# Transposing attention probabilities in halves of 64 queries, and taking the value products one pair of heads later

## The reference

```python
for i in range(S // BLOCK):                      # two blocks of 128 queries
    q0, e = i * BLOCK, (i + 1) * BLOCK
    s = jnp.einsum('bqhd,bkhd->bhqk', q[:, q0:e], k[:, :e]) * scale
    s = s + c[:, :, q0:e, None] - c[:, :, None, :e]        # a bias for each head
    p = jax.nn.softmax(jnp.where(causal, s, NEG), axis=-1)
    outs.append(jnp.einsum('bhqk,bkhd->bqhd', p, v[:, :e]))
# y = concat(ya * silu(ga), yb * silu(gb));  x + y @ w_out
```

## Time and profile before

| | |
|---|---|
| median of 3 runs | 768.49 us (768.45 to 770.68) |
| profiled execution | 769.24 us, span 767.4 us |
| PE busy | 759.1 us of the span, 99% |
| DVE, ACT, POOL busy | 69%, 54%, 29% |
| granted TensorE clock | 0.998 of full speed |
| the two stretches of `attend_gated` | about 121.6 to 140.1 us and 215.5 to 233.9 us |
| attention of the third layer | about 521 to 539 us |

### The profile page before, as it was taken

One profiled execution on the slowest core, in us unless ns is written; L12 is line 12 of the kernel. 1 busy time (PEld: TensorE's weight loads), 2 busy tenths in 40 slices (PEclk: granted clock), 3 DMA queues, 4 the chain that ended last, 5 costly groups with the idle time before them and its releaser, 6 DMA issues.

```text
span 767.4 us, 12161 instructions
## 1 busy us (share of the span) xinstructions
PE 759.1 (99%) x4802; PEld 647.4 (84%) x4802; DVE 528.3 (69%) x793; ACT 417.4 (54%) x678; POOL 222.7 (29%) x175
## 2 busy tenths in 40 slices
PE   9999999999999999999999999999999999999997
PEld 7888887899877889887778888998888888888885
DVE  5876876755577557975567865788788676667553
ACT  6675458443696454453344554727857555456451
POOL 2113993730940000064029900126012111011010
PEclk9999999999999999999999999999999999999999
DMA  8989886578622745455435565430465656655741
GB/s 263 234 191 270 266 191 181 128 178 198 157 62 81 240 141 193 160 197 161 141 110 164 193 219 167 142 133 29 163 194 158 184 174 199 196 189 165 244 167 55
DMA packets 79064, 131.98 MB, mean 172 GB/s; under 512 B 4656, under 2 KB 28496, under 8 KB 79008
## 3 DMA queue, kind: packets, MB, share of 16 engines
q1 hardware_dynamic: 77072, 126.01, 55.9%
q0 software_dynamic: 1648, 5.09, 2.3%
q10 hardware_dynamic: 288, 0.11, 0.1%
HBM read 130.12 MB, written 1.06 MB: 171 GB/s over the span
## 4 chain that ended last, share of the span: by engine, by line
PE 98%; DVE 1%; issue 0%; ACT 0%; DVEq 0%; ACTq 0%
PE ps L1765 16%; PE ps L1769 15%; PE ps L1773 15%; PE ps L1840 10%; PE ps L1822 7%; PE ps L1848 5%; PE ps L1827 3%; PE ps L1806 3%; PE ps L1810 3%; PE ps L1802 3%; PE ps L1915 2%; PE ps L1931 2%; PE ps L1946 2%; PE ps L2304 1%; PE ps L2181 1%; PE ps L2133 1%
## 5 line engine op out<-in xcount | busy, mean ns | idle before, releaser
L1067 DVE TENSOR_TENSOR w_lo<-stage,w_hi 128x1024 fp32r<-128x1024 f32 x224 | 292.3, 1330 | 136.9 <-ACT w_hi L688 136.0
L688 ACT ACTIVATE w_hi<-stage 128x1024 fp32r<-128x1024 f32 x230 | 239.2, 1060 | 213.5 <-PE ps L1773 103.7
L1765 PE MATMUL ps<-w_hi,act_t 128*128 128x512 f32 (+1 forms) x368 | 100.5, 396 | 0.2 <-ACT act_t L715 0.2
L1773 PE MATMUL ps<-w_lo,act_t 128*128 128x512 f32 (+1 forms) x368 | 96.5, 385 | 0.0
L1840 PE MATMUL ps<-act_t,w_hi 128*128 128x512 f32 x352 | 84.1, 391 | 0.0
L1773 PEld LDWEIGHTS ps<-w_lo,act_t 128*128 128x128 f32 x368 | 68.1, 188 | 14.0
L1769 PE MATMUL ps<-w_hi,act_t 128*128 128x512 f32 (+1 forms) x304 | 79.4, 384 | 0.0
L1765 PEld LDWEIGHTS ps<-w_hi,act_t 128*128 128x128 f32 x368 | 66.5, 188 | 15.1 <-issue 2.5
L1840 PEld LDWEIGHTS ps<-act_t,w_hi 128*128 128x128 f32 x352 | 64.7, 188 | 12.7
L1769 PEld LDWEIGHTS ps<-w_hi,act_t 128*128 128x128 f32 x304 | 56.1, 188 | 11.6
L1822 PE MATMUL ps<-act_t,w_hi 128*128 128x512 f32 x224 | 56.5, 394 | 0.0
(11 more groups left out here) (399 smaller groups left out, 1248.3 us busy)
## 6 DMA issues: line engine op xcount, KB each, us to landing
stage<-in_even_w_in SPq DMA_DIRECT2D x62, 512.0 KB, 5.4
stage<-in_odd_w_in SPq DMA_DIRECT2D x48, 512.0 KB, 4.5
stage<-in_w_gate_up SPq DMA_DIRECT2D x44, 512.0 KB, 4.7
stage<-in_w_down SPq DMA_DIRECT2D x22, 512.0 KB, 4.3
stage<-in_even_w_out SPq DMA_DIRECT2D x16, 512.0 KB, 4.4
stage<-in_odd_w_out SPq DMA_DIRECT2D x16, 512.0 KB, 4.0
stage<-in_w_in SPq DMA_DIRECT2D x10, 512.0 KB, 3.7
stage<-in_w_out SPq DMA_DIRECT2D x8, 512.0 KB, 4.7
```

The lines of the kernel that those rows point to most:

```text
L688: nc.scalar.activation(w_hi[:, u % RING, :], stage[:, u % RING, :], ACT.Copy).then_inc(hi_ready, 1)
L1067: nc.vector.tensor_tensor(w_lo[:, u % RING, :], stage[:, u % RING, :], w_hi[:, u % RING, :].bitcast(F32), ALU.subtract).then_inc(lo_ready, 1)
L1765: mm(out[:, b, :], a_hi(k)[:, tok[b]], hi[:, i, :], start=(k == 0), stop=False)
L1773: ins = mm(out[:, b, :], a_hi(k)[:, tok[b]], lo[:, i, :], start=False, stop=(k == k_tiles - 1))
```

## The change

Each transpose of 128 queries is cut into two of 64 queries: rows 0 to 63 and rows 64 to 127 of the slot are the weights of two transposes in the 64*128 division, the one that the scores use, and they land in two banks side by side. Both heads of a pair share these two banks. One copy then takes both heads of a pair (768 columns, `slots_of_pair` from `turned_pair`) on one engine: ACT has pairs 3, 5 and 7 of a half and DVE the other five; in the third layer ACT has pairs 0 and 2, DVE pairs 1 and 3. The order in `attend_gated` becomes: turn pair i, scores of pair i+4, values of pair i-2. The gates' transposes keep their place behind the scores, and so now stand behind the turning of the same step. There are eight slots instead of six, and the tile `wf_both` moves into the shared work area to make room.

```diff
-SLOTS = 6
+SLOTS = 8
-COPIED_BY_ACT = (1, 3, 5, 7, 9, 13, 15)
+PAIRS_BY_ACT = (3, 5, 7)
@@ sizes and places
-            return (6 if n < FOX_H + DIL_H and n % 16 < 2 else 2) + n % 2
+            return 6 if n < FOX_H + DIL_H and n % 16 < 2 else 2
+        def turned_half(n, m, h):
+            at = (turned_at(n) + h) * BANK + m * 192
+            return ps[:, at:at + 192].rearrange("p (a q) -> p a q", a=3)
+        def turned_pair(n):
+            both = ps[:, turned_at(n) * BANK:(turned_at(n) + 2) * BANK].rearrange("p (h c) -> p h c", h=2)
+            return both[:, :, 0:384].rearrange("p h (a q) -> p a h q", a=6)
+        def slots_of_pair(n):
+            two = prob_slots[:, n % SLOTS:n % SLOTS + 2, :].rearrange("p m c -> p (m c)")
+            return two.rearrange("p (a h q) -> p a h q", a=6, h=2)
@@ ACT
-                copy_prob_act(16 * half + 1)
                 for n in range(16 * half + 4, 16 * half + 16):
-                    if copied_by_act(n - 2):
-                        copy_prob_act(n - 2)
+                    if n % 2 == 1 and copied_by_act(n - 3):
+                        copy_prob_act(n - 3)
                     exponentials(n)
                     if n % 16 == 11:
                         copy_gates(4 * half)
                 copy_gates(4 * half + 1)
-                copy_prob_act(16 * half + 15)
+                copy_prob_act(16 * half + 14)
-            copied_behind = {33: 32, 37: 34, 38: 36}
+            copied_behind = {33: 32, 38: 36}
-            copy_prob_act(38)
@@ DVE
                     if i >= 3 and i % 2 == 1:
-                        for m in (n - 3, n - 2):
-                            if not copied_by_act(m):
-                                copy_prob(m)
+                        if not copied_by_act(n - 3):
+                            copy_prob(n - 3)
@@ PE
+            def turn_pair(n):
                 if n >= 2 and turned_at(n) == turned_at(n - 2):
                     wait_copied(pe, n - 2)
+                for m in range(2):
+                    pe.wait_ge(exped, n + m + 1)
+                    for part in range(3):
+                        for h in range(2):
+                            r = slice(h * P // 2, (h + 1) * P // 2)
+                            ins = nc.tensor.transpose(turned_half(n, m, h)[:, TURNED_PART_AT[part], :], prob_slots[r, (n + m) % SLOTS, part * P:(part + 1) * P], ident[r, r])
@@ attend_gated
-                    if 0 < i and i + 2 < 16:
-                        scores_of_pair(n + 2, (q_of(i + 2), q_of(i + 3)), (k_of(i + 2), k_of(i + 3)))
                     if i == 2:
                         values_there()
+                    if i < 16:
+                        turn_pair(n)
+                    if i + 4 < 16:
+                        scores_of_pair(n + 4, (q_of(i + 4), q_of(i + 5)), (k_of(i + 4), k_of(i + 5)))
                     if i == 10:
                         turn_gates(first // 4)
                     if i == 14:
@@
                     if i >= 2:
                         values_of_two(n - 2, v_of)
-                    if i < 16:
-                        turn_prob(n)
-                        turn_prob(n + 1)
```

More of the change, by code:

```diff
@@ L198, in build @@
         W_F = P // 2
-        wf, wf_both = sb("wf", [P, KD * FOX_H]), sb("wf_both", [P, (KD + 1) * W_F], F32R)
-        wf_part = lambda at: wf_both[:, 0:KD * W_F].rearrange("p (k c) -> p k c", c=W_F)[:, :, at:at + FOX_H]
+        wf = sb("wf", [P, KD * FOX_H])
         wf_of = wf[:].rearrange("p (k h) -> p k h", k=KD)
@@ L227, in build @@
         junk = over("junk", 10240, [P, NB, D])
+        wf_both = over("wf_both", 11264, [P, (KD + 1) * W_F], F32R)
+        wf_part = lambda at: wf_both[:, 0:KD * W_F].rearrange("p (k c) -> p k c", c=W_F)[:, :, at:at + FOX_H]
         q0, k0, v0 = over("q0", 0, [P, 8, S]), over("k0", 2048, [P, 8, S]), over("v0", 4096, [P, NB, 1024])
@@ L371, in turned_at @@
         def turned_at(n):
-            return (6 if n < FOX_H + DIL_H and n % 16 < 2 else 2) + n % 2
+            return 6 if n < FOX_H + DIL_H and n % 16 < 2 else 2
[8 more added lines that the diff above has]
+            return two.rearrange("p (a h q) -> p a h q", a=6, h=2)
         def copied_by_act(n):
-            return n % 2 == 0 if n >= FOX_H + DIL_H else n % 16 in COPIED_BY_ACT
+            pair = n // 2
+            return pair % 2 == 0 if n >= FOX_H + DIL_H else pair % 8 in PAIRS_BY_ACT
         def wait_copied(eng, n):
-            done = sum(copied_by_act(i) == copied_by_act(n) for i in range(n + 1))
+            done = sum(copied_by_act(i) == copied_by_act(n) for i in range(0, n + 1, 2))
             eng.wait_ge(prob_copied_act if copied_by_act(n) else prob_copied, done)
@@ L824, in copy_prob_act @@
             def copy_prob_act(n):
-                act.wait_ge(prob_turned, n + 1)
-                nc.scalar.activation(prob_slots[:, n % SLOTS, :], bank(turned_at(n), 384), ACT.Copy).then_inc(prob_copied_act, 1)
+                act.wait_ge(prob_turned, n + 2)
+                nc.scalar.activation(slots_of_pair(n), turned_pair(n), ACT.Copy).then_inc(prob_copied_act, 1)
             def take_lower(name, dst):
@@ L1290, in copy_prob @@
             def copy_prob(n):
-                dve.wait_ge(prob_turned, n + 1)
-                nc.vector.tensor_copy(prob_slots[:, n % SLOTS, :], bank(turned_at(n), 384)).then_inc(prob_copied, 1)
+                dve.wait_ge(prob_turned, n + 2)
+                nc.vector.tensor_copy(slots_of_pair(n), turned_pair(n)).then_inc(prob_copied, 1)
             def invert(g):
@@ L1546, in _ @@
                 score_max(33 + i, 2)
-                if i >= 2:
-                    copy_prob(32 + i - 1)
+                if i == 4:
+                    copy_prob(34)
                 if i % 4 == 2:
@@ L1554, in _ @@
                 invert_sinks(g)
-            copy_prob(39)
+            copy_prob(38)
             scale_heads(0)
@@ L1918, in scores_of_pair @@
                 odd.then_inc(scores, 1)
-            TURNED_PART_AT = (P, 2 * P, 0)
-            def turn_prob(n):
-                pe.wait_ge(exped, n + 1)
+            TURNED_PART_AT = (1, 2, 0)
+            def turn_pair(n):
                 if n >= 2 and turned_at(n) == turned_at(n - 2):
@@ L1928, in turn_prob @@
                     pe.wait_ge(b_ready, 8)
[L1929 to L1932, removed]
+                for m in range(2):
[4 more added lines that the diff above has]
+                            ins = nc.tensor.transpose(turned_half(n, m, h)[:, TURNED_PART_AT[part], :], prob_slots[r, (n + m) % SLOTS, part * P:(part + 1) * P], ident[r, r])
+                            if (m, part) == (1, 2):
+                                ins.then_inc(prob_turned, 1)
             def values_of_two(n, v_of):
-                for m in range(n, n + 2):
-                    wait_copied(pe, m)
+                wait_copied(pe, n)
                 i = n // 4
```

## The result

The changed kernel takes 773.73 us (median of 6, 772.81 to 774.75) against 768.62 us for the kernel before in the same comparison (6 runs, 768.45 to 770.68): a ratio of 1.0064, 95% interval 1.0050 to 1.0077. It is slower, by 5.1 us; the forecast was +3.3 us and 771.8 us. A second comparison gave 1.0064 again (1.0052 to 1.0077).

A forecast was written before the change was run, and what follows sets the result against it. PE, busy for 99% of the span, was taken as the bound. Two halves at +2.0 us each and the third layer at -0.7 gave +3.3 on 768.49: 771.8 us, own range 770.5 to 773.5, 8-in-10 range 766.5 to 775.5.

The forecast's parts named there:

- The price of a turning: PE's transposes of a pair: twelve small ones take 0.35 us instead of 0.65, and one change of array division goes.
- Rival 1: In turning, weight loads pace the half transposes, 0.68 us a turning: +5.1 us, 773.6 us; chance 0.12.
- rival 2: In turning, the two row halves don't run side by side, 1.31 us a turning: 785 us; chance 0.03.
- The floor of 2.22 us a round: Attention rounds: the single pair of score banks allows 2.22 us, down from 2.46, whatever turning costs.
- The head: Start of each half: scores 6 wait for DVE's maxima of head 5, so PE waits 1.6 us.
- The gates: First gate, turned behind turning 10: ACT stands 2.4 us, and PE waits 1.6, then 0.6 us around turning 12.
- The tail: End of each half: turning 14 waits 0.5 us for DVE's copy of pair 6 and exponential 15.
- rival 3: Gate and head waits are half as long, or the gate goes ahead of turning 10: no change told, 768.6 us; 0.22.
- The half: Each attention half: PE waits of 5.4 us (0.3 before) against 3.1 us less work, +2.0 us.
- the method: Written engine orders laid against each other with durations; for the order of before, next projection at 139.9, trace 140.07.
- The third layer: Its attention: four turnings save 0.3 to 0.4 us each, values wait for later pair copies; -0.7 us.
- Rival 4: ACT's gate copy isn't held up and rounds of 2.22 last: 1.7 us gained a half, 764.4 us; chance 0.15.

The follow-up runs named there:

- late_gate_first: The changed kernel with the first gate's transposes of each half moved ahead of the turning of heads 10 and 11: 770.04 us, ratio 1.0002 to the kernel before.
- after_again: The changed kernel unaltered, measured and profiled once more: 774.51 us, ratio 1.0064 to the kernel before.
- after_busy: The changed kernel with six unread 128x128 products on PE before turning 12 of each half: 773.47 us, ratio 1.0057 to the kernel before.
- late_copy_later: The changed kernel with ACT's copy of each half's first gate behind exponential 13 instead of 11: 768.33 us, ratio 0.9987 to the kernel before.
- before_again: The kernel before, unchanged, run once more for its trace: 770.01 us in a single execution.
- early_split11: The kernel before, its order and six slots kept, with transposes of 64 queries and every pair's copy split between DVE and ACT: 764.79 us, ratio 0.9940.
- before_stall2: The kernel before with ACT copying each half's first gate five times, each repeat waiting for the last: 772.73 us, ratio 1.0042.

## Why the prediction was right, and where it was off

**The price of a turning: right.** It said 0.35 us and one change of division less, 0.40 in all and 0.39 less than before with its change; the timeline has 0.42 to the scores behind it. Eight times 0.39 is 3.1 us, as the prediction had. The trace's busy time falls by only 1.7 us a half (18.17 to 16.47), and its idle time rises by 3.3 and not 5.1: where scores wait briefly for their banks, turning and scores lie 0.56 us apart (127.69 to 128.25) and the trace marks no idle time. So the split into work saved and waits can't be checked to the last 1.5 us, only their sum. The forms of the transposes give the loads that it bounded:
```profile
L1947 PEld LDWEIGHTS ps<-ident,prob_slots x240: 134/138/142, 123.2 to 540.1; 64*128 64x128 f32 x120
L1947 PE MATMUL ps<-ident,prob_slots x240: 216/223/276, 123.2 to 540.1; 64*128 64x64 f32 x120
```
A load lasts 138 ns, hardly less than the 140 of a whole transpose, so that far the rule of the Trainium skill in "TensorE: Matmul & The Clock Gate" holds: fewer rows make no shorter load. But the loads of the two row halves overlap, and twelve transposes with their loads take no longer than 0.42 us. Rival 1, loads as the pace, would need 0.68, and falls with rival 2.

**The floor of 2.22 us a round: right.** Rounds are 2.21 to 2.23 us, and in the best version, whose order is that of before, 2.21 and 2.22 once the lead is used up. The one round of 2.09 us shows that PE's own work is less, and scores start 0.06 us after DVE's last maxima (128.53 to 128.59): the pair of score banks paces the loop, and a still cheaper turning would only lengthen that wait.

**The head: right in kind, 0.4 too long.** The wait was 1.22 us and not 1.6.

**The gates: right.** ACT's wait is 2.43 us (2.4 forecast), PE's are 1.46 and 0.47 (1.6 and 0.6). The tail has 0.28 in place of 0.5. `late_gate_first` gave what rival 3 said of that variant, no change to be told: 1.0002.

**The half: the mechanism right, the size +1.57 and +1.70 in place of +2.0.** The named waits sum to 3.6 us (with 0.16 at scores 14) where the prediction's summed to 4.3, the head's most of all (1.22 for 1.6). In part the method put the half of before 0.2 us too short, which it had shown itself.

**The third layer:** -0.77 for -0.7. Values 34 still wait 0.36 us for the pair's copy, as expected:
```profile
536.57 0.65 PE L1962 MATMUL ps<-prob_slots,qkv 128*64 128x256 f32 x4 [0.36 <-DVE prob_slots L1307]
...
543.25 0.98 PE L1779 MATMUL ps<-w_hi,act_t 128*128 128x512 f32 x3
```

**The term that was missing: the clock.** The prediction costed at full clock what stands behind the waits. With the stages as measured at full clock the sum is +1.57 + 1.70 - 0.77 = +2.5 us; with both halves slowed, as in `after_again`, it is +4.9. Over the executions a low clock goes with less than that, 774.5 against 773.2 us. So the median of 773.73 us came out 0.2 above the forecast's own range of 770.5 to 773.5 while the stages came out 0.8 below its +3.3: an overestimate of the stages and two costs outside the sum, the clock and what is named below, partly made up for each other, and that is luck. What makes the clock fall is open. Low clocks were frequent where PE stood for 1.2 to 1.5 us at turning 12 (18 of 23 executions of three kernels), but 2 of 6 executions of `after_busy` and 1 of 11 of `late_copy_later` had them without that wait.

**What stays open.** At full clock the changed kernel still has 773.2 us, 3.4 above the kernel before in the second comparison and 4.6 above it in the first, where the stages give +2.5. The spans of the two profiles differ by 4.5 us, and the traces say where:

| us | before | after | difference |
|---|---|---|---|
| up to the first turning | 121.59 | 123.16 | +1.57 |
| the two halves | 36.83 | 40.10 | +3.27 |
| between the halves | 75.47 | 75.57 | +0.10 |
| second half to the third layer's scores | 287.30 | 287.55 | +0.25 |
| third layer's attention | 17.64 | 16.87 | -0.77 |
| rest | 228.57 | 228.65 | +0.08 |

The first row differs from profile to profile: the first turning stands between 120.83 and 124.07 us in the fourteen of them, 121.59 and 122.45 in the two of the kernel before, 123.16 and 121.41 in the two of the changed one. PE waits for a late low part near 108 us in eight of them (0.57 to 1.09 us, 0.98 in the profile after, 0.78 in `before_again`), and up to 0.55 us for units within the first 10 us in several; whether the change makes this more frequent, single profiles don't tell. The 0.10 us between the halves stands in every profile with halves of 64 queries and in none without; its cause is open.

**Rival 4** priced its case wrongly. With ACT's hold-up gone (`late_copy_later`) a half gains 0.55 us and not 1.7, because the head's wait of 1.22 us stays, which that sum had left out. Its 764.4 us are reached without that wait, in the old order with split copies: `early_split11` has 764.79, and gains 2.0 us a half.

## What to carry to other kernels

A reordering that gives one engine more lead is judged by what it does to the single instruction that doesn't belong to the loop. Here the rounds got 0.25 us shorter, and one gate, turned 2.4 us too late for the engine that copies it, took more than that back; turning it one block earlier restored 1.6 us a half, and copying it two exponentials later 2.1. When a step becomes cheaper, try it in the old order first, and split the copy that follows between two engines by bank: that gave 764.79 us. And where a schedule makes the matrix engine stand, look at the granted clock in several executions, since a profile at full clock may be the rarer case, as it was here (3 of 12).

## What the runs showed of the hardware

- Transposes of 64 queries in the two row halves overlap almost wholly: twelve with the change to scores take 0.42 us, six of 128x128 take 0.81. Scores in the same division start at 123.58, while the records of the transposes run on to 123.75.
- A load of 64 rows lasts 138 ns and one of 128 rows 140; an ordinary load of as many columns lasts 187 (`L2181`).
- The granted clock went to half for about 3 us behind waits of 1.46 and 0.47 us in `after_again`, and mean clocks of 0.997 or less came in 9 of 12 executions of that kernel. None came with waits of 0.72 and 0.33 us (6 executions of `before_stall2`), nor in 11 of `late_gate_first` with 1.22 us at the head and 0.22, 0.47 and 0.28 later.
- The clock differs between executions of one kernel: without the wait of 1.46 us it was low in 2 of 6 (`after_busy`) and 1 of 11 (`late_copy_later`).
